# Prompt attention of a decoder step: head inputs requested in a new order, keys made for two heads at once, modulation chunks in four partition groups

## The reference: what is computed

```python
shift1, scale1, gate1, shift2, scale2, gate2 = split(silu(c) @ w_mod + b_mod)   # w_mod 1024 x 6144, 9 rows of c
h = rmsnorm(x, g_mix) * (1 + scale1) + shift1
u, cq, ckv, kr = split(h @ w_in)
q = rmsnorm(cq, g_q) @ w_uq          # 8 heads of 64 + 32 columns; the 32 are rotated
lat = rmsnorm(ckv, g_kv)
k_nope = lat @ w_uk                  # 64 columns a head; k_rope (32 columns) is shared by all heads
v = lat @ w_uv
s = (q_nope @ k_nope.T + q_rope @ k_rope.T) / sqrt(96), causal
o = softmax(s) @ v
x = x + gate1 * (concat(pool_out, o) @ w_out)
x = x + gate2 * (relu(h2 @ w_up) ** 2 @ w_down)
```

## Time and profile before

| | |
|---|---|
| median of 3 runs | 1682.05 us (1679.85 to 1682.74) |
| the profiled execution | 1680.51 us, of which its span is 1678.4 us |
| PE busy | 1543.8 us (92% of the span) |
| DVE, ACT, POOL busy | 688.9, 430.0, 400.5 us |
| chain that ended last | PE 82%, DVE 7%, DMA 5% |

### The profile page before, as it was taken

How to read it: one execution, slowest core, us unless ns; L and a number is a source line. 1 busy time by engine, 2 the same in 40 slices (tenths; PEclk the granted TensorE clock), 3 DMA queues, 4 the chain that set the end, 5 groups by cost and what they waited for, 6 DMA issues and landing times.

```text
span 1678.4 us, 23761 instructions
## 1 busy us (share of the span) xinstructions
PE 1543.8 (92%) x9793; PEld 1356.0 (81%) x9793; DVE 688.9 (41%) x1456; ACT 430.0 (26%) x911; POOL 400.5 (24%) x308
## 2 busy tenths in 40 slices
PE   4369967998997999999999999999999999999998
PEld 3169956655555766666899999999999999999997
DVE  2862184444443444344476432323233232323245
ACT  3321134443443233333123202020110102020134
POOL 0510330222222211113220606050421406050300
PEclk9679988999998999999899999999999999999999
DMA  9510112123124444443400302020110203020102
GB/s 321 189 59 1 52 66 91 62 78 107 62 79 160 155 164 148 168 161 107 153 13 13 101 1 90 12 81 21 51 51 13 89 1 88 13 76 26 38 1 107
DMA packets 91530, 137.18 MB, mean 82 GB/s; under 512 B 15867, under 2 KB 65991, under 8 KB 87191
## 3 DMA queue, kind: packets, MB, share of 16 engines
q1 hardware_dynamic: 80431, 85.07, 15.7%
q0 software_dynamic: 7872, 46.14, 7.7%
q10 hardware_dynamic: 3120, 4.46, 0.8%
HBM read 121.98 MB, written 13.79 MB: 81 GB/s over the span
## 4 chain that ended last, share of the span: by engine, by line
PE 82%; DVE 7%; DMA 5%; issue 2%; ACT 2%; POOLq 1%; SPq 1%; DVEq 0%; POOL 0%; ACTq 0%
PE psa L1236 23%; PE psa L1250 22%; PE psa L1214 6%; PE psa L1086 4%; PE psa L1113 4%; DMA qh<-q_scr 3%; PE psa L1153 3%; PE psa L838 3%; PE psa L431 3%; PE psa L821 3%; PE psa L961 2%; PE psa L1116 2%; DVE sqb L411 1%; PE psa L982 1%; PE psa L943 1%
## 5 line engine op out<-in xcount | busy, mean ns | idle before, releaser
L1236 PE MATMUL psa<-hhi,wr 128*128 128x384 f32 (+1 forms) x1536 | 374.5, 326 | 0.0
L1236 PEld LDWEIGHTS psa<-hhi,wr 128*128 128x128 f32 x1536 | 270.9, 188 | 0.1
L1250 PE MATMUL psa<-g_hi,wd_hi 128*128 128x384 f32 (+1 forms) x768 | 251.3, 327 | 0.0
L1236 PE MATMUL psa<-hlo,wr 128*128 128x384 f32 (+1 forms) x768 | 250.3, 326 | 0.0
L1250 PE MATMUL psa<-g_hi,wd_lo 128*128 128x384 f32 (+1 forms) x768 | 250.3, 326 | 0.0
L1250 PE MATMUL psa<-g_lo,wd_hi 128*128 128x384 f32 (+1 forms) x768 | 250.2, 326 | 0.0
L2043 DVE SCALAR_TENSOR_TENSOR xT<-psa,modT,xT 128x384 f32<-128x384 f32 (+1 forms) x216 | 123.1, 571 | 191.6 <-PE psa L1250 160.9
L1630 ACT ACTIVATE g_relu<-psa 128x384 f32<-128x384 f32 (+1 forms) x96 | 45.4, 473 | 600.9 <-PE psa L1236 600.9
L609 POOL TENSOR_SCALAR wr<-wraw 128x1024 fp32r<-128x1024 f32 x34 | 36.4, 1070 | 562.3 <-PE psa L1236 491.9
L2108 DVE TENSOR_TENSOR psa<-psa,g_relu 128x384 f32<-128x384 f32 (+1 forms) x96 | 52.2, 544 | 261.6 <-ACT g_relu L1630 261.6
L1236 PEld LDWEIGHTS psa<-hlo,wr 128*128 128x128 f32 x768 | 144.1, 188 | 0.1
(11 more groups left out here) (329 smaller groups left out, 2572.2 us busy)
## 6 DMA issues: line engine op xcount, KB each, us to landing
wmod<-in_w_mod SPq DMA_DIRECT2D x8, 2048.0 KB, 8.2
wraw<-in_w_up SPq DMA_DIRECT2D x32, 512.0 KB
wraw<-in_w_down SPq DMA_DIRECT2D x32, 512.0 KB
wmod<-in_w_mod POOLq DMA_DIRECT2D x4, 2048.0 KB, 12.9
x_scr<-xT SPq DMA_DIRECT2D x1, 4352.0 KB, 19.3
xstage<-in_x_prompt SPq DMA_DIRECT2D x8, 512.0 KB, 8.5
wraw<-in_w_out SPq DMA_DIRECT2D x8, 512.0 KB
out_y_p<-yst SPq DMA_DIRECT2D x8, 512.0 KB, 2.9
```

What stands on the lines that cost most here:

```text
L1236: mm = pe.matmul(out[:, :N], w[:, c * P:c * P + P], x[:, c, c0:c0 + N], start=(c == 0 and q == 0), stop=(c == KD - 1 and q == 2))
L1250: mm = pe.matmul(out[:, :N], w[:, c, n * P:n * P + P], x[:, c, c0:c0 + N], start=(c == 0 and q == 0), stop=(c == FG - 1 and q == 2))
```

## The change

Five edits, taken from the diff:

1. The order of SP's loads in stage 3. `head_in` only loads queries; a new `pair_in(p)` loads the key weights of two heads. The wait on `kr_lo` ahead of the first modulation load is gone, and the key weights of the second pair go first.
2. `make_k(m)` makes half the keys (512) of two heads with 128 output rows, at t = 3 alone, one head in each of the first six; `k_hi` and `k_lo` copy its two halves by two instructions each. Four key buffers in place of two.
3. The rotated key part is copied once ahead of the first scores and three times in head 0 (i = 3, 5, 7).
4. A modulation chunk goes to one of four groups of 32 PSUM rows (c % 4), its stationary operand is padded from 9 to 32 columns, one ACT copy of 128 rows takes the place of two of 9, and `pick` has 128 rows. In stage 3 the chunks stand at t = 6 and 7, four each.
5. Buffers are moved to make room; a padded copy `silu2` is made at the end of stage 2.

```diff
-    def mod_matmuls(pe, w, out, chunks=range(KD)):
+    def mod_matmuls(pe, silu, w, out, chunks=range(KD)):
         for c in chunks:
-            rows = slice(32 * (c % 2), 32 * (c % 2) + 9)
-            mm = pe.matmul(out[rows, :], siluT[:, c, :], w[:, c, :], start=(c < 2), stop=(c >= KD - 2))
+            rows = slice(32 * (c % 4), 32 * (c % 4) + 32)
+            mm = pe.matmul(out[rows, :], silu[:, c, :], w[:, c, :], start=(c < 4), stop=(c >= 4))
...
+        def pair_in(p):
+            if p >= 1:
+                sp.wait_ge(sem("wuk_split"), p)
+            sp.dma_start(wuk_raw[:, :, :], w_uk.rearrange("(k p) n -> p k n", p=P)[:, :, 2 * p * DN:2 * p * DN + 2 * DN])\
...
-        sp.wait_ge(sem("kr_lo"), 1)
-        mods_in(0)
-        for hh in range(1, H):
-            head_in(hh)
+        for hh in range(H):
+            if hh >= 1:
+                head_in(hh)
+            if hh % 2 == 0 and hh + 2 < H:
+                pair_in(hh // 2 + 1)
             mods_in(hh)
...
-            if t == 0 and hh + 1 < H:
-                split_wuk(hh + 1)
+            if t == 0 and hh % 2 == 0 and hh + 2 < H:
+                split_wuk(hh // 2 + 1)
...
-                    mm = pe.matmul(out[0:DN, :], a[:, c, :], x[:, c, 512 * w:512 * w + 512],
+                    mm = pe.matmul(out[:, :], a[:, c, :], x[:, c, 512 * w:512 * w + 512],
...
-            if t in (3, 4) and hh + 1 < H:
-                make_k(hh + 1, t - 3)
+            if t == 3 and hh + 2 < H:
+                make_k(hh + 2)
             if t == 5:
                 values(hh, 0, range(4))
-                mods(hh, (0, 1))
             if t == 6:
-                mods(hh, (2, 3, 4))
+                mods(hh, range(4))
             if t == 7:
-                mods(hh, (5, 6, 7))
+                mods(hh, range(4, KD))
...
-            act.activation(modrow[0:9, n % 2, :], bank(4 + n % 2)[0:9, :], ACT.Copy)
-            act.activation(modrow[32:41, n % 2, :], bank(4 + n % 2)[32:41, :], ACT.Copy).then_inc(sem("mod_row"), 1)
+            act.activation(modrow[:, n % 2, :], bank(4 + n % 2), ACT.Copy).then_inc(sem("mod_row"), 1)
...
+            for u in range(2):
+                act.activation(kT_hi[0:DN, (2 * p + u) % 4, 512 * w:512 * w + 512],
+                               bank(3 if p else w)[u * DN:u * DN + DN, :], ACT.Copy).then_inc(sem("k_hi"), 1)
...
+            if i in (3, 5, 7):
+                rope_hi((i - 1) // 2)
```

More of the change, by code:

```diff
@@ L181, in build @@
     A2 = sm("A2", [P, KD, 9])
[L182 removed]
     eps = sm("eps", [P, 1])
[L184 removed]
+    pick = sm("pick", [P, 9])
     idx = sm("idx", [P, NB, 5], U32)
@@ L1005, in mods @@
                 pe.wait_ge(sem("wmod2_in"), 16 * hh + 16)
-                if hh + 1 < H:
-                    pe.wait_ge(sem("k_lo"), 2 * hh + 4)
+                if hh + 2 < H:
+                    pe.wait_ge(sem("k_lo"), 2 * hh + 6)
+                elif hh + 1 < H:
+                    pe.wait_ge(sem("q_lo"), 2 * hh + 4)
                 else:
                     pe.wait_ge(sem("mod_ev"), 4 + hh)
-            mm = mod_matmuls(pe, wmod2, bank(3), chunks)
+                if hh == 0:
+                    pe.wait_ge(sem("silu"), 2)
+            mm = mod_matmuls(pe, silu2, wmod2, bank(3), chunks)
             if chunks[-1] == KD - 1:
@@ L1019, in _ @@
             turn_q(0, w)
-        for w in range(2):
-            make_k(0, w)
-        pe.wait_ge(sem("kr_lo"), 1)
+        for m in range(2):
+            make_k(m)
         scores(0)
@@ L1441, in _, with rope_hi @@
         barrier(act, 2)
-        for u in range(2):
+        def rope_hi(u):
             act.activation(kT_hi[DN:DQ, u, :], krr[DN:DQ, 0:TP], ACT.Copy).then_inc(sem("kr_hi"), 1)
@@ L1486, in _ @@
             q_hi(0, w)
-        for w in range(2):
-            k_hi(0, w)
+        for m in range(2):
+            k_hi(m)
+        rope_hi(0)
         exponentials(0)
@@ L1504, in _ @@
                 act.wait_ge(sem("mod_mm"), hh + 5)
-                act.activation(modrow[0:9, 0, :], bank(3)[0:9, :], ACT.Copy)
-                act.activation(modrow[32:41, 0, :], bank(3)[32:41, :], ACT.Copy).then_inc(sem("mod_row"), 1)
+                act.activation(modrow[:, 0, :], bank(3), ACT.Copy).then_inc(sem("mod_row"), 1)
             if i + 2 < NT:
@@ L1829, in _, with rope_lo @@
             v.tensor_copy(v_all[:, t, :], bank(2 + t % 2)).then_inc(sem("v_ev"), 1)
-        v.memset(modrow[:, 0, :], 0.0)
+        chain(v.memset(silu2[:, :, :], 0.0))
+        v.tensor_copy(silu2[:, :, 0:9], silu_keep[:, :, :]).then_inc(sem("silu"), 1)
         barrier(v, 2)
         v.memset(pt0[:, 1, 0:P], 0.0)
-        for u in range(2):
+        def rope_lo(u):
             v.wait_ge(sem("kr_hi"), u + 1)
-            kr = tt(kT_lo[DN:DQ, u, :], krr[DN:DQ, 0:TP], kT_hi[DN:DQ, u, :].bitcast(F32), ALU.subtract)
-        kr.then_inc(sem("kr_lo"), 1)
+            tt(kT_lo[DN:DQ, u, :], krr[DN:DQ, 0:TP], kT_hi[DN:DQ, u, :].bitcast(F32), ALU.subtract)\
+                .then_inc(sem("kr_lo"), 1)
         def q_lo(hh, w):
@@ L1845, in q_lo, with k_lo @@
              .then_inc(sem("q_lo"), 1)
-        def k_lo(hh, w):
-            cols = slice(512 * w, 512 * w + 512)
-            v.wait_ge(sem("k_hi"), 2 * hh + w + 1)
-            tt(kT_lo[0:DN, hh % 2, cols], bank(3 if hh else w)[0:DN, :], kT_hi[0:DN, hh % 2, cols].bitcast(F32), ALU.subtract)\
-                .then_inc(sem("k_lo"), 1)
+        def k_lo(m):
+            p, w = m // 2, m % 2
+            for u in range(2):
+                dst = (2 * p + u) % 4, slice(512 * w, 512 * w + 512)
+                v.wait_ge(sem("k_hi"), 2 * m + u + 1)
+                tt(kT_lo[0:DN, dst[0], dst[1]], bank(3 if p else w)[u * DN:u * DN + DN, :],
+                   kT_hi[0:DN, dst[0], dst[1]].bitcast(F32), ALU.subtract).then_inc(sem("k_lo"), 1)
         def the_rest(i):
@@ L1891, in _ @@
             q_lo(0, w)
-        for w in range(2):
-            k_lo(0, w)
+        for m in range(2):
+            k_lo(m)
+        rope_lo(0)
         maximum(0)
@@ L1906, in _ @@
                 q_lo(hh + 1, t - 1)
-            if t in (3, 4) and hh + 1 < H:
-                k_lo(hh + 1, t - 3)
+            if t == 3 and hh + 2 < H:
+                k_lo(hh + 2)
+            if i in (3, 5, 7):
+                rope_lo((i - 1) // 2)
             if t == 5:
```

74 lines of the change are left out of this document (39 added, 35 removed).

## The result

The changed kernel takes 1675.01 us (1672.95 to 1678.16, 6 runs) against 1683.34 us (1679.85 to 1688.87, 6 runs) before: the ratio is 0.9949, with a 95% interval of 0.9929 to 0.997. It is 8.3 us faster, where 31.8 were forecast, and lies outside the range given. The profiled execution took 1674.98 us, its span is 1673.2.

The account below looks back on a forecast made before the run. Each stage 3 head was taken as a load latency of some 9.6 us plus 21.2 us of PE work. Gains summed to 31.8: 1680.5 to 1648.7, as a median about 1650, range 1643 to 1664.

Parts of the forecast that it names:

- B: Modulation chunks: four groups are no faster than two, total gain 18.0 us, so 1664 us; chance 0.13.
- E: Modulation chunks: groups of 32 columns run one record at a time, net 15.5 us slower, 1698 us; chance 0.02.
- The start of stage 3: PE takes the first late queries at 287.4 instead of 289.76: 2.4 us gained, bounds 1.0 and 2.9.
- the keys: Key matmuls on PE: heads 0 to 5 lose one group of 1.42 us, of which PE keeps 1.1.
- head 6: Stage 3, no key halves left: 2.84 + 2.73 less 0.5 makes 5.0 us gained.
- What the softmax gives back: Heads 1 to 5: of 4.15 us taken from PE 0.75 goes back, 3.4 a head, 17.0 for five.
- Head 0: Stage 3, with rotated copies at i = 3 and 5 ahead of maxima: 0.6 us gained.
- Head 7: Stage 3, last turn waits on the chain from maximum(7), 0.35 earlier at most: 1.5 us gained.
- Stage 1: Modulation blocks 0 to 3 and the ACT copy behind them: 1.7 + 3.3 + 0.3 us gained.
- The first term: Stage 1, blocks 0 and 1: only the first block's saving gets through, 1.7 us, bounds 0 and 3.4.
- Rival C: Stage 3: the softmax decides every head, ACT and DVE later than walked; gain 22.3 us, 1660 us; chance 0.13.
- something unforeseen that eats the gain: Whole kernel: a cause not named in the forecast removes the gain; chance 0.04.

Follow-up runs that it names:

- `first_four` early: Changed kernel with ACT's copy first_four(i) put ahead of exponentials(i + 2): 1651.16 us, ratio 0.9819 to the kernel before.
- the store held: Changed kernel with SP's 4.35 MB store of x_scr held until the fourth modulation load has landed: 1669.42 us, ratio 0.9916 to the kernel before.
- the queries ahead: Kernel before with SP issuing the queries of the head after next ahead of each modulation load: 1659.52 us, ratio 0.9868.

## Why the prediction was wrong

**What was right.** Four groups run side by side: eight chunks 1.9 us, four chunks 1.06 (1.03 taken), blocks 2 and 3 4.84 once their data are there (4.8 worked out). Rivals B and E fall, and with B its reading of program order record by record: that gives 9 slots of 0.43 for eight chunks, and four groups took 4. Whole chunks may still start in order; no row here shows otherwise. By the Trainium skill (TensorE: Matmul & The Clock Gate, Part 3, "Measured speedup vs the span model") three column tiles gave 2.38 times the speed of one; this case shows two against four, 3.56 against 1.9, a factor of 1.9, and no sign of a limit below four. The start of stage 3 gained 2.4 us (12.9 to 10.5) as forecast, and the first scores came 1.4 later (1.25 taken). PE's idle time ahead of the queries stayed, since SP's order had not changed what it waits for: 16.6 us in six heads. Before, it was 2.38 to 3.65 a head and 20.7 in all, where the prediction has 2.6 to 3.7 and 22; it goes with the other order, and gives 21 to 23. From the queries to `values` heads 1 to 5 gave 0.8 each, 1.1 forecast for the keys; no run tries the keys alone.

**Right by luck: head 6.** It gave 6.5 (33.63 to 27.12), 5.0 forecast, but from other places. From the queries to `values` it gave 4.6 (13.28 to 8.71), where 2.84 stood for the keys, and the queries landed 1.1 sooner behind SP's issue. The chunks, 2.2 of the forecast, gave 0.8, all behind `turn(6)`; from `values` to `turn(6)` it is 7.26 and 7.23.

**The step that failed is "What the softmax gives back".** The walk through heads 1 to 5 followed POOL's scaling to `turn(6)` and found a wait of 0.5. It left out the other thing that `turn(6)` waits for, the PSUM bank that `first_four(5)` clears behind `exponentials(7)`. In the walk's own head, head 3, the scaling was over at 402.95 + 1.01 = 403.96 and the copy at 405.70. Worked through, the trace of before had said so. Behind the `maximum(7)` of the earlier trace rows it has:

```profile
399.95 1.11 ACT L1482 ACTIVATE prob<-psa,nmx 128x1024 f32<-128x1024 f32 x1 [2.38 <-DVE nmx L1887]
...
401.05 0.59 ACT L1466 ACTIVATE pt<-psa 128x512 f32<-128x512 f32 x1
...
401.79 0.96 PE L982 MATMUL psa<-ident,prob 128*128 128x128 f32 x7
```

398.69 and 1.23 for the maximum, 1.11 for the exponential and 0.59 for the copy put `turn(6)` no earlier than 401.62; it stood at 401.79. The walk moved this maximum by 0.35 only, so by its own numbers `turn(6)` was at 401.4 and not at 399.3: 2.1 a head, 10.7 of the 17.0. No step of this chain waits for the chunks any more, so their whole gain at t = 5 and 6 became waiting. The low level of the clock behind the wait took the gain at t = 7, some 1.5 us in each of four of the five heads, 6.2. These two estimates leave 0.1 of the 17.0, and heads 1 to 5 gave 1.3. Shown: with the copy in front of the exponential the same kernel has heads of 27.4 us and runs in 1651.16. The prediction named "a PSUM or buffer hand-over that I read as free" as what would make it wrong, but looked for it at bank 3; the longest wait of PE there is 0.3 us.

By the Trainium skill (TensorEngine Tiling (Array Packing), "PSUM Bottleneck") tiling speeds up TensorE and not the emptying of PSUM, so that a PSUM copy may become the bottleneck. The trace agrees in kind: eight waits, 17.3 us, for a copy of 0.59. It was its place in ACT's written order, though, and not its length.

**Head 0.** 0.6 to be gained, but from the turned queries to SP's next issue it went from 21.76 us (289.76 to 311.52) to 25.26 (290.49 to 315.75): 3.5 lost, with the same wait, 3.52 long, and one of 1.88 for POOL that I had at 0.3. With `first_four` early the stretch is 21.41; the wait for POOL at `turn(4)` stays. With the rotated copies of i = 5 and 7 moved it is 23.05, and from `values` to `turn(6)` 7.33 in place of 9.04: in head 0 they cost about 2 us, on ACT and DVE ahead of the chain that `turn(6)` waits for. In the whole kernel this gain isn't seen.

**Head 7.** 1.5 forecast. From SP's last issue to the last `values` it is 26.0 us (496.31 to 522.35) against 25.8 before: nothing, by the same chain, which had cost it a wait of 0.76 before already.

**Stage 1** failed in its condition. 1.7 + 3.3 + 0.3 were forecast, and 1.3 came (40.3 to 39.0 from the first block to A). The prediction took the modulation loads as in time, without a look at the one that was nearly late; it was early by 0.6 us before and held PE 3.24 after, and the chunks behind the wait took 3.52 us in place of 1.9. The first term was too small: up to block 2 the changed kernel gained 3.2, near the bound of 3.4. With the store held the stage gives 6.5 us in the trace, 5.2 of them new, and the time fell by 5.6.

**The sum**, in the profiled executions, with the forecast in brackets: stage 1 1.3 (5.3), start 2.4 (2.4), head 0 -3.5 (0.6), heads 1 to 5 1.3 (17.0), head 6 6.5 (5.0), head 7 -0.2 (1.5): 7.8 of 31.8, near the 8.3 of the medians. The two executions differ by 5.5 only. The first block began 2.7 us later (26.02 against 23.28), which isn't the change: the kernel before with the queries ahead has the same stage 1 and its first block at 25.24. Another 1.7 was lost between A and stage 3 and some 2 won behind stage 3; these were not followed up.

**The clock.** The prediction tied the low level to waits of 3.3 us or more and left it out of the sum. Head 4 of the kernel before waited 2.38 us and stands at 0.94 all the same, so that size doesn't decide it, and the change brought a new wait, 1.82 to 1.94 us ahead of `turn(6)`, with the low level behind it in four of five heads.

**The chances.** 0.95 on faster held. Rival C had the right kind of cause, ACT and DVE late, and gave 1660 since it still counted 2.0 a head; "something unforeseen that eats the gain" had 0.04, too little for a walk through five engines in which only one of two waits at each `turn` was looked at.

## What to carry to other kernels

When work is taken from the engine that looks busy, list every semaphore that its next instruction waits for, and follow each one through the written order of the engine that signals it, not only the one that was nearest before: a chain that is as long as the work beside it (7.25 us here, where PE alone needs 7.01) can't be seen in the waits, and takes the whole gain. A short copy that hands a buffer back belongs in front of long work that waits for something else. For a load, take the latency of that one transfer beside what runs next to it, and not the median, and write the slack down.

## What the runs showed of the hardware

- With work taken from PE, its clock fell (head 4: 0.94 to 0.89). In head 4 of the changed kernel PE, idle 1.82 us ahead of `turn(6)`, had a granted clock of 0.57 from there to `turn(7)`, near the lower of its two levels, 1.2 GHz, and four chunks took 1.94 us there in place of 1.06. The wait alone doesn't decide it: head 3's was 1.94, and its four chunks behind it took 1.07, at 406.73. With the wait gone (`first_four` early) the same stretch is at 1.00.
- A load of 2 MB took 10.8 us at best in stage 1, and 26.4 beside a store of 4.35 MB; with the store held back the longest took 16.5.
- Four groups of 32 PSUM rows halve the time of two for these float32 chunks, which stand as two records each: 1.9 against 3.56 us for eight.
